# Softmax turns as products with diagonals, and the gated keys' exponentials on ScalarE alone, in a three-mixer network on one core

## The reference

```python
p = jax.nn.softmax(jnp.concatenate([s, sink], axis=-1), axis=-1)[..., :-1]
o = jnp.einsum('bnhgqk,bnkhd->bnqhgd', p.astype(v.dtype), vv)
```

```python
rel = b[:, :, :, None, :] - b[:, :, None, :, :]
decay = jnp.where(causal, jnp.exp(jnp.minimum(rel, 0.0)), 0.0)
sc = jnp.einsum('bhid,bhijd,bhjd->bhij', qi, decay, ki)
```

## Time and profile before

| | us |
|---|---|
| median of 3 runs | 2097.81 |
| lowest, highest | 2092.47, 2097.97 |
| the profiled execution | 2095.14 |
| its span in the trace | 2093.2 |
| TensorE, VectorE, ScalarE busy in the span | 1994.0, 1088.8, 932.5 |

### The profile page before, as it was taken

How to read it: one execution, slowest core, us unless ns; L and a number is a source line. 1 busy time by engine, 2 the same in 40 slices (tenths; PEclk the granted TensorE clock), 3 DMA queues, 4 the chain that set the end, 5 groups by cost and what they waited for, 6 DMA issues and landing times.

```text
span 2093.2 us, 25307 instructions
## 1 busy us (share of the span) xinstructions
PE 1994.0 (95%) x9881; PEld 1488.5 (71%) x9881; DVE 1088.8 (52%) x2023; ACT 932.5 (45%) x1737; POOL 12.6 (1%) x28
## 2 busy tenths in 40 slices
PE   8999889999889999899999999999999999999997
PEld 4876446687447788566788888777666668888885
DVE  5623764632874422657656543442386575565333
ACT  3733664643674233564422322344587543233223
POOL 1000000000000000000000000000000000000000
PEclk8999889999989999999999999999999999999998
DMA  8431432123202433003233333415400123333331
GB/s 287 122 87 51 161 101 81 54 79 91 81 21 81 148 94 86 16 1 116 71 100 92 101 93 94 116 53 125 146 2 1 51 71 101 96 95 98 94 94 48
DMA packets 301268, 183.13 MB, mean 87 GB/s; under 512 B 17551, under 2 KB 292109, under 8 KB 299949
## 3 DMA queue, kind: packets, MB, share of 16 engines
q1 hardware_dynamic: 295437, 166.05, 27.4%
q10 hardware_dynamic: 4704, 13.31, 1.7%
q0 software_dynamic: 1008, 2.15, 0.3%
HBM read 179.22 MB, written 2.27 MB: 87 GB/s over the span
## 4 chain that ended last, share of the span: by engine, by line
PE 84%; DVE 8%; ACT 5%; issue 1%; DMA 1%; another core or an unknown queue 0%; ACTq 0%; DVEq 0%
PE PS L903 22%; PE PS L905 22%; PE PS L904 22%; PE PS L1049 3%; PE PS L1077 2%; PE PS L1062 2%; PE PS L1203 1%; DVE WLO L2080 1%; DVE SE L2154 1%; ACT WHI L1515 1%; PE PS L1226 1%; PE PS L1121 1%; PE PS L1015 1%; DVE X L2047 1%; PE PS L1130 1%
## 5 line engine op out<-in xcount | busy, mean ns | idle before, releaser
L904 PE MATMUL PS<-LO,WHI 128*128 128x512 f32 x1690 | 659.4, 390 | 0.0
L903 PE MATMUL PS<-HI,WHI 128*128 128x512 f32 x1578 | 626.2, 397 | 23.7 <-DVE LO L2053 9.2
L905 PE MATMUL PS<-HI,WLO 128*128 128x512 f32 x1578 | 616.0, 390 | 0.0
L2080 DVE TENSOR_TENSOR WLO<-RING,WHI 128x1024 fp32r<-128x1024 f32 (+3 forms) x271 | 314.3, 1160 | 530.1 <-ACT WHI L1515 529.1
L1515 ACT ACTIVATE WHI<-RING 128x1024 fp32r<-128x1024 f32 (+3 forms) x271 | 272.6, 1007 | 469.0 <-PE PS L905 446.7
L903 PEld LDWEIGHTS PS<-HI,WHI 128*128 128x128 f32 x1578 | 297.2, 188 | 105.7 <-issue 27.1
L904 PEld LDWEIGHTS PS<-LO,WHI 128*128 128x128 f32 x1690 | 318.4, 188 | 65.1 <-issue 1.7
L905 PEld LDWEIGHTS PS<-HI,WLO 128*128 128x128 f32 x1578 | 297.1, 188 | 63.0
L903 PE MATMUL PS<-HIDDEN,WHI 128*128 128x512 f32 x352 | 137.1, 390 | 0.6 <-PE PS L905 0.6
L905 PE MATMUL PS<-HIDDEN,WLO 128*128 128x512 f32 x352 | 137.0, 389 | 0.0
L904 PE MATMUL PS<-HIDDEN,WHI 128*128 128x512 f32 x352 | 136.9, 389 | 0.0
(11 more groups left out here) (333 smaller groups left out, 2302.7 us busy)
## 6 DMA issues: line engine op xcount, KB each, us to landing
RING<-in_ffn_w_up SPq DMA_DIRECT2D x88, 512.0 KB, 3.8
RING<-in_w_in SPq DMA_DIRECT2D x48, 512.0 KB, 3.9
RING<-in_w_mod SPq DMA_DIRECT2D x32, 512.0 KB, 4.1
RING<-in_ffn_w_down SPq DMA_DIRECT2D x32, 512.0 KB, 4.0
RING<-in_ev_w_in SPq DMA_DIRECT2D x30, 512.0 KB, 4.0
RING<-in_w_out SPq DMA_DIRECT2D x16, 512.0 KB, 4.5
RING<-in_od_w_in SPq DMA_DIRECT2D x15, 512.0 KB, 4.0
RING<-in_ffn_w_down SPq DMA_DIRECT2D x16, 384.0 KB, 3.4
```

The source lines that it names most:

```text
L903: mm(bank, WHI[i2][:, i, :], hi, start=(k == 0), stop=False)
L904: mm(bank, WHI[i2][:, i, :], lo, start=False, stop=False)
L905: return mm(bank, WLO[i2][:, i, :], hi, start=False, stop=last)
L2080: tt(WLO[i2][:, 0:nk, :], raw, WHI[i2][:, 0:nk, :], ALU.subtract).then_inc(me.signals(w_split), 1)
```

## The change

ScalarE no longer multiplies the exponentials of a head pair by the reciprocals. It writes two 128x128 diagonal matrices, the identity times the reciprocal of each row, into a new view DIAG of the tile S. TensorE's turn becomes a float32 product of each block of exponentials with the diagonal in place of a transpose against the identity; the product is the turned and scaled block. The semaphores of this lane stay as they are.

In the gated attention VectorE's subtraction into GKEY goes, and with it the semaphore keys_to_exp. ScalarE computes exp(reference - running sum) by itself, in eight instructions of 128x128 with the reference as bias and -1 as scale, straight from the running sum BT. VectorE's product with the keys waits for all eight. From qb = 2 on ScalarE first waits until TensorE has done the own-block product that last read that buffer of GKEY.

```diff
+        DIAG = S.rearrange("p a t -> p (a t)")[:, 1544:2312].rearrange("p (r a q) -> p r a q", r=3, a=2)
...
                         for c in range(nb):
-                            ins = nc.tensor.transpose(PS[:, 4, (a * nb + c) * B:(a * nb + c + 1) * B],
-                                                      pair_e(i % 3, a, 2 * B)[:, c * B:c * B + B], IDN)
+                            ins = mm(PS[:, 4, (a * nb + c) * B:(a * nb + c + 1) * B],
+                                     pair_e(i % 3, a, 2 * B)[:, c * B:c * B + B], DIAG[:, i % 3, a, :], start=True, stop=True)
                     ins.then_inc(swa_turned, 1)
...
                 def normalise(i):
-                    n, r = todo[i]["n"], i % 3
+                    r = i % 3
                     act.wait_ge(swa_recip, n0 + i + 1)
                     for a in range(2):
-                        e = pair_e(r, a, n)
-                        fn(e, e, ACT.Copy, scale=RDEN[:, 2 * r + a:2 * r + a + 1]).then_inc(me.signals(swa_probs), 1)
+                        fn(DIAG[:, r, a, :], IDN, ACT.Copy, scale=RDEN[:, 2 * r + a:2 * r + a + 1]).then_inc(me.signals(swa_probs), 1)
...
                 def within(qb):
-                    act.wait_ge(keys_to_exp, me.after(keys_to_exp))
-                    fn(GK2[qb % 2], GK2[qb % 2], ACT.Exp).then_inc(me.signals(keys_exp), 1)
+                    if qb >= 2:
+                        act.wait_ge(gla_own, NB * l + qb - 1)
+                    for a in range(8):
+                        fn(GK2[qb % 2][:, a, :], z(BT)[:, qb * B:qb * B + B], ACT.Exp, bias=BREF[:, 8 * qb + a:8 * qb + a + 1], scale=-1.0) \
+                            .then_inc(me.signals(keys_exp), 1)
...
                     dve.wait_ge(*me.last)
-                    tt(GK2[qb % 2], BREF[:, 8 * qb:8 * qb + 8].unsqueeze(2).broadcast_to([P, 8, B]), heads(bb, 8), ALU.subtract) \
-                        .then_inc(me.signals(keys_to_exp), 1)
                     tt(GPROD[qb % 2].rearrange("p c (a j) -> p c a j", a=8), within(bb), over(bb), ALU.subtract) \
                         .then_inc(me.signals(gla_to_act), 1)
...
-                    dve.wait_ge(keys_exp, me.after(keys_exp))
+                    dve.wait_ge(keys_exp, me.after(keys_exp, 8))
```

More of the change, by code:

```diff
@@ L330, in build @@
         gla_to_act, gla_to_pe, gla_act = sem("gla_to_act"), sem("gla_to_pe"), sem("gla_act")
-        keys_to_exp, keys_exp, keys_ready = (sem(n) for n in ("keys_to_exp", "keys_exp", "keys_ready"))
+        keys_exp, keys_ready = sem("keys_exp"), sem("keys_ready")
         swa_scores, swa_scaled, swa_exp, swa_recip, swa_probs, swa_turned, swa_turn_free, swa_values, swa_mixed = (
```

## The result

The changed kernel takes 2106.18 us in the median (2102.36 to 2112.21, eight runs), the kernel before, run beside it, 2095.71 us (2092.02 to 2098.53, eight runs). The ratio is 1.0056 with a 95% interval of 1.0044 to 1.0067, so the change makes the kernel slower by some 11.7 us (10.5 us between the medians). The forecast was slower by 23 us, 2118 us in a range of 2103 to 2131: the sign and the range hold, the size is twice what came. The profiled execution took 2107.02 us with a span of 2104.8, 11.6 us above the span of before.

The account below looks back on a forecast made before the run. The prediction took the mixing stages to be bound by a ring of TensorE, ScalarE and VectorE handing work on. Quarters added 12.2 us in layer 1 and 10.8 in layer 0: 2095.1 + 23 = 2118 us, range 2103 to 2131.

Parts of the forecast that it names:

- The turns' instructions: TensorE's turns: a full turn goes from 4 to 8 instructions, +0.59 us at the upper clock level, +1.04 at the lower.
- rival (d): TensorE's turns: a product's second pass costs little, turns grow half as much, 2111 us; chance within the forecast's shared 0.66.
- The turns' term: Every TensorE turn in the two layers' chains doubles: 6.2 + 7.2 = 13.4 us, ends 10.3 and 29 us.
- the diagonals' 2.2: ScalarE's narrower diagonal writes end a pair 0.22 us earlier; six pairs in layer 1's chain, five in layer 0's.
- The keys' step: ScalarE's eight key exponentials start 0.30 us apart, 2.4 us against 0.95 before: +1.45 us a quarter.
- the keys' term: Longer key exponentials on ScalarE delay the quarters: 5.0 us in layer 1 and 3.7 in layer 0, together 8.7.
- the freed subtraction: VectorE loses 1.22 us a quarter, almost everywhere slack; only layer 0's first quarter gains, a 0.40 us ScalarE wait.
- the wait for the w_mod transfer: Layer 0's second quarter: this 5.6 us wait moves along, covering the keys and the short turn; quarter +1.0 us.
- Rival (a): Mixing stages: TensorE's clock stays up, up to 21.4 us come back, 2094 us, no change; chance 0.10.
- Its reason against: Mixing stages: the lulls stay, being waits for VectorE's and ScalarE's work, and ScalarE's gets longer; no size given.
- Rival (c): Clock turns against the change: layer 1's first quarter loses 6 us, another lull falls, 2127 us; chance 0.16.

Follow-up runs that it names:

- e2: Kernel before with only the keys' exponentials moved to ScalarE, turns and their scaling unchanged; 2099.72 us, 1.0035 of the kernel before.
- f4: Changed kernel with the keys' exponentials of blocks 1 to 3 issued a quarter earlier; 2097.91 us, 1.0020 of the kernel before.

## Why the prediction was right in sign and twice too large

**The turns' instructions: right.** Groups by form of the stage of layer 0, kernel after (busy us, mean ns, idle before):

```profile
L1131 PE MATMUL PS<-S,E 128*128 128x128 f32 x112 | 19.8, 325 | 12.4 <-ACT S L1723 12.4
...
L1723 ACT ACTIVATE S<-MATS,TINY 128x128 f32<-128x128 f32 x32 | 11.0, 393 | 5.2 <-DVE TINY L2228 5.2
L1763 ACT ACTIVATE GKEY<-Z,BIAS 128x128 f32<-128x128 f32 x32 | 9.7, 388 | 0.0
L2315 DVE SCALAR_TENSOR_TENSOR GKEY<-GKEY,Z 128x1024 f32<-128x1024 f32 x4 | 4.9, 1223 | 3.4 <-ACT GKEY L1763 3.4
```

112 in place of 56, and a full turn is eight in 1.16 us at the upper level, as L1162's eight in the earlier trace rows. That refutes rival (d), by which they would take 0.9. At the lower level, here in layer 1's second quarter, eight take 2.07, a little under twice the 1.11 of four.

```profile
579.74 2.07 PE L1131 MATMUL PS<-S,E 128*128 128x128 f32 x8
```

**The turns' term of 13.4 us, net 11.2 with the diagonals' 2.2: too high.** At one clock it is 6.4 to 8.3 us. The low end of the prediction, 70 instructions of the chains all at the upper level, was 10.3 less 2.2, 8.1 us, and that is where it lies. I had taken the sum of the pieces as they stood, those at the lower level included. The quarters of the prediction add up to still more: they come to 23 us, of which the keys are 8.7 (5.0 in layer 1 and 3.7 in layer 0, as e2's expectation has them), so that 14.3 are the turns less the diagonals. The 3.1 us beyond 11.2 are mostly single turns at the lower level (1.04, 1.06, 1.1) and copies that wait for them. It is this term that was most mis-sized, by 6 to 8 us.

**The keys' step: right; the keys' term: too high.** Eight exponentials take 2.34 us from the first's start to the next instruction's (590.47 to 592.81), VectorE's product waits 1.23 us for them, and the freed subtraction is slack. But in the sum they stood for 8.7 us. Measured alone, in e2, the quarters grow by 3.9 us and the median by 7, at the same mean clock; and with three quarters of the loss taken off either side of the profiles, the eight quarters change by -0.3, +0.1, +0.1 and +1.4 in layer 0 and +1.3, +0.6, +0.7 and +1.3 in layer 1, 5.2 us. Where the clock is 1.00 on both sides nothing has to be taken off: 40.71 to 41.99 us in layer 1's first quarter, the 1.3 to 1.45 I had priced, and 17.90 to 18.00 in layer 0's second, where the wait for the w_mod transfer covered them as I had written. I had let them pass on in full in layer 0's first and third and in layer 1's second and third quarters, there with 0.35 us for the next diagonals besides. Why they don't pass there isn't shown.

**The clock: the step that failed for the turns.** Rival (a) had 0.10. Its reason against was that the lulls stay and ScalarE's part gets longer. The waits do stay, and get longer:

```profile
PEld PS L1131 <- ACT S L1723: 19.1, 10, 4.2
...
DVE GKEY L2315 <- ACT GKEY L1763: 3.4, 3, 1.2
```

These are the waits in layer 1's quarters of the kernel after (us in total, times, longest). The first of the two is, before, the line

```profile
PEld PS L1130 <- ACT E L1723: 15.0, 10, 2.8
```

What the reason missed is that more work beside a wait can count, whatever the wait does. The keys' part is the reason's case, and there it holds: the mean clock stays at 0.978. The turns' part is the rival's case: it rises to 0.984, and TensorE's weight loads wait for the diagonals ten times in layer 1 as before, 14.0 us in place of 15.0. Together they stand at 0.979 to 0.980, hardly above before. The turns win the clock, and with the keys in place nearly all of it is gone; that their longer wait for the diagonals is what takes it is argued, and f4 bears it out, where the exponentials stand elsewhere and the clock is 0.982. This is why two parts that cost 0 and 7 us alone cost 12 to 14 together (ratios 1.0056 and 1.0065): together they cost what they cost at one clock.

**The sum put right.** The forecast had 14.3 us for the turns less the diagonals and 8.7 for the keys, +23. At one clock the first measured 6.4 to 8.3 us and the second 5.2 to 7, together 12 to 15. The changed kernel took 11.7 us more than before in its first group and 14.7 in its second, where the mean clocks are equal. So over the repeated runs the terms alone account for the time, and the clock gives back little, at most three quarters of some 2 us. Of the 8 to 11 us by which the forecast missed, 6 to 8 are the turns and 2 to 3.5 the keys. The two profiles taken by themselves tell it otherwise: the quarters are 8.0 us longer, 14.5 with three quarters of the loss taken off on either side, and 6.5 us would be the clock's. That is this pair, with before at 0.976. The forecast was built on that execution and added to its time, so what most other executions have back without any change can't be put down to it. How much of each quarter's rise was the change and how much the execution stays open, for want of a second profile of before.

**The range.** Its lower end, 2103, was (d) with a third of (a); (d) is false and (a) was true for one of the two parts and lost again in the whole, so the time lies inside for a reason that the range didn't name, and that is in part luck. Rival (c) didn't come as a whole, but one quarter shows it: layer 0's third fell from 0.90 to 0.83 and grew by 2.2 us.

## What to carry to other kernels

Where the windows show a granted clock below 1.00 around waits, added work on TensorE isn't priced by its durations alone: work it out twice, with the clock as it stands and with it at 1.00, and give the second case a real chance. Price apart what adds work to TensorE and what makes it wait; here the first was free and the second was not, and together they cost more than their sum. Read the clock from many executions before a profile of one is made the base: here the one profiled stood at 0.976 where most stand near 0.979, some 6 us of clock loss. And where TensorE waits for another engine in such a stage, a few transposes of a constant in the wait are a cheap thing to try: 88 of them took 0.36% off this kernel, though the same 88 did nothing for the changed one, whose waits lie elsewhere.

## What the runs showed of the hardware

- Repeating transposes raised the granted clock as much as exchanging them for products: the mean of whole executions went from 0.979 to 0.984 in both, over twelve runs each. The Trainium skill's "TensorE: Matmul & The Clock Gate", part on PE-mode transpose, would have transposes leave it down; here 112 more of them went with a rise from 0.84 to 1.00 in layer 1's fourth quarter. A third copy brought the mean back to 0.980.
- The clock's falls in a stage can repeat: in two profiled executions, in separate groups of runs, the changed kernel showed the same granted clock in all eight quarters, to two places. The mean clock of a whole execution still varies, from 0.975 to 0.982 in 72 executions of the kernel before.
- A float32 product of a 128x128 tile costs two instructions of 0.147 us, a transpose one; at the lower level 0.26 us each.
- A small ScalarE instruction with a scale or bias from a tile starts every 0.30 us at 128 columns: eight in 2.34 us, against 0.95 us for one instruction on all 1024 columns. Splitting it cost 1.4 us a quarter, more than VectorE's 1.22 us that it saved, and it was ScalarE that TensorE waited for.
